# A two-layer hybrid decoder step on one core: the front part of a layer reordered on ScalarE, VectorE and GpSimd

## The chip, the cores and the metric

The kernel runs on one core of one Trainium2 chip. The metric is the device time in microseconds (us) of one execution of the whole program. Before the change the median of three runs is 1627.45 us (1622.06 to 1631.64). PE is TensorE's matmul stream, PEld its weight loads, DVE is VectorE, ACT is ScalarE, POOL is GpSimd, SP is SyncE.

## What is computed

A token stream of 256 prompt tokens and 8 sequences of 8 sample tokens (T = 320 columns together) passes through two layers. Each layer normalises, projects, runs three mixers side by side, merges them under sigmoid gates, and ends in a SwiGLU block:

```python
z = rms_norm(x) @ w_in            # xr | cq | ckv | kpe | u | v | merge gates
# recurrence (RG-LRU)
r, i = sigmoid(xc @ wa + ba), sigmoid(xc @ wx + bx)        # xc: 4-tap convolution of xr
log_a = -8 * r * softplus(-lam); a = exp(log_a)
h[t] = a * h[t-1] + sqrt(-expm1(2 * log_a)) * (i * xc)
# latent attention
q = rms_norm(cq) @ w_uq; q_nope = rms_norm(...); q_pe = rope(rms_norm(...))
latent = rms_norm(ckv); k_pe = rope(rms_norm(kpe)); k_nope, v = expand(latent)
p = softmax((q_nope.k_nope + q_pe.k_pe) * scale)           # prompt: causal; sample: 16 pages of 128 cached rows
# spatial gating
s = tril(w_s) @ layer_norm(gelu(v)); y = gelu(u) * s        # gelu by tanh
x = x + sum(sigmoid(g) * proj(branch)) @ w_out; x = x + swiglu(rms_norm(x))
```

gelu's tanh argument is sqrt(2/pi) * (x + 0.044715 x^3).

## The kernel before

Activations are held feature-major, 128 partitions by T columns a tile. Nearly all products are made from high and low halves (three matmuls for one), so every streamed weight unit (`raw`, 128x1024) is first copied to `w_hi` on ACT (`split` in the ACT program) and subtracted into `w_lo` on DVE (`split` in the DVE program), in three rotating slots. A unit of 24 matmuls of 320 columns takes PE some 3.6 us; the weights come over SP's queue.

The order on each engine is written out by hand. Each engine has a program of its own, waits on semaphores (`wait_ge`) and raises them (`then_inc`), and runs strictly in its own order. PSUM has eight banks; PE takes a bank once whoever reads it has released it (`release`, a drain and an increment).

A layer runs through these stages: `project` (19 weight units, the normalisations, the gates of the recurrence, query and key products), `spatial_and_attention_inputs`, `prompt_attention` (8 heads, the spatial product between them), `pages` (8 sample sequences over 16 pages, a loop, the longest stage), then the merge rounds and the FFN. "Front part" below means the first three. In layer 0 they take 0 to 149 us of the span, in layer 1 815 to 953 us, and a landmark of layer 1 lies 804.3 us behind that of layer 0.

What the change touches, in the order of the front part (lines of the kernel before, as the profile gives them; every ACT instruction is recorded under the helper's line 1303, and ACT's release under 1307, DVE's under 1754):

- ACT, `project`: after `split(12)` come the latent's high half `lat_hi`, `split(13)` to `split(16)`, `recurrence_tanh(0..3)` (two tanh of 320 columns out of banks 4 to 7, each with a release), `query_tile` (copy and square out of PSUM, banks 1, 2, 3, 0), two rotary tiles, the gelu square and tanh of v (`ge`), the recurrence's second tanh and exponential (`mu`, `tr`), a table load, `split(17)`, `split(18)`, the two logarithms of the recurrence, the logarithms and roots of the query norms (`qrs`), the recurrence's square root (`mu`), and the square of the centred v (`varsq`). Then, in the next stage, the four key copies (`kT`, `ksq`).
- DVE: `split`, `scaled` (PSUM times the token's scale, and a release), the rotary key (L1872 to L1876), the input of the recurrence (L1878), v's gelu (L1882), the floor of the recurrence's tanh at 1e-30 (L1884, `lru_clamped`), the difference of logarithms (L1890), the centring (L1893), the scaled queries `qz` (L1902), the recurrence with its scan (L1908 to L1924), the copy of the absorbed queries `qabs` (L1928), the rotary query scaled (L1934) and rotated (L1941 to L1946), the scaled keys (L1948).
- POOL: gelu's argument in two steps (`gelu_argument`, L634 and L636), once for v and once for u; the split of the key weights into `comb_hi` and `comb_lo` (L643, L645), output DMAs, clearing `qz` (L656), copies of identity and mask (L663, L665), half of the rotary queries by head `qpz` (L672), the masking of the new scores (L687, L690).
- PE at the end of `project`: key products (L908), the sum of squares of v (L835, `var_mm`), the absorbed queries (L921, banks 4 and 5, `abs_mm`), the sums of squared keys (L928, `kstat`, banks 0 to 3), the rotation of the queries (L934, banks 4 and 5, `qrot_mm`), the value products (L942), the new scores (L961). In `prompt_attention` L1019 transposes the probabilities that DVE has normalised (L1999 to L2002).

## Time and profile before

| | us | share of the span |
|---|---|---|
| median of three runs | 1627.45 | |
| the profiled execution, its own time | 1621.21 | |
| its span, first to last instruction | 1619.4 | |
| PE busy | 1573.2 | 97% |
| PEld busy | 1522.0 | 94% |
| DVE busy | 1061.5 | 66% |
| ACT busy | 885.0 | 55% |
| POOL busy | 532.2 | 33% |

In forty slices of the span PE is busy nine tenths or more nearly everywhere; the slices below that are the first (7 tenths) and the ones from 121 to 162 us and from 931 to 972 us (8 tenths each). Matmuls are pipelined, so "busy" is not "at its peak": a small hesitation between two of them can hide in it. In a timeline a row is a run of equal instructions, with its start, how long it took, its count, and in brackets the idle time of its engine before it and who ended it.

### The profile page before, as it was taken

The page shows a single profiled execution, that of the slowest core. Times are in us where ns is not written, and L with a number is a line of the kernel's source. Part 1 is how long each engine was busy: PE and PEld are TensorE (multiplying, and loading weights), DVE is VectorE, ACT ScalarE, POOL GpSimd, SP SyncE. Part 2 cuts the span into 40 slices and gives each one's busy share as a digit, 9 for nine tenths or more (in the row PEclk, how much of TensorE's full clock was granted, in tenths as well). Part 3 has the DMA queues.
Part 4 walks back from the last instruction along what each step waited for, and adds up shares of the span by engine and source line. Part 5 has one row for each costly group of instructions (what it writes and reads, how often), then busy time and mean ns, then how long its engine had stood idle before and what let it go on. Part 6 is the DMA issues. An engine that isn't in the chain of part 4 may idle for free. (4 is left out here: it accounts for less than half of the span.)

```text
span 1619.4 us, 33228 instructions
## 1 busy us (share of the span) xinstructions
PE 1573.2 (97%) x10860; PEld 1522.0 (94%) x10860; DVE 1061.5 (66%) x1619; ACT 885.0 (55%) x1612; POOL 532.2 (33%) x667
## 2 busy tenths in 40 slices
PE   7998999999999999999999989999999999999999
PEld 7877999999899999999998779999998999999999
DVE  6586767777555766664375867677775647666633
ACT  5676676667533454443357766766774344544432
POOL 3742367776520000000048413777675000000000
PEclk9999999999999999999999999999999999999999
DMA  7331455554544444444453314555535344444443
GB/s 269 117 106 40 130 183 157 161 158 125 157 141 146 146 154 144 154 147 154 143 192 96 103 57 135 184 156 162 161 115 172 125 156 146 148 149 151 147 150 116
DMA packets 114690, 232.90 MB, mean 144 GB/s; under 512 B 12881, under 2 KB 78706, under 8 KB 114450
## 3 DMA queue, kind: packets, MB, share of 16 engines
q1 hardware_dynamic: 112178, 223.13, 44.4%
q0 software_dynamic: 2400, 8.36, 1.5%
q8 instruction: 60, 0.98, 0.3%
q14 instruction: 52, 0.43, 0.1%
HBM read 228.98 MB, written 2.46 MB: 143 GB/s over the span
## 5 line engine op out<-in xcount | busy, mean ns | idle before, releaser
L1760 DVE TENSOR_TENSOR w_lo<-raw,w_hi 128x1024 fp32r<-128x1024 f32 x258 | 319.4, 1240 | 236.9 <-ACT w_hi L1303 234.5
L1303 ACT ACTIVATE w_hi<-raw 128x1024 fp32r<-128x1024 f32 x258 | 272.0, 1056 | 336.4 <-PE PS L808 322.3
L808 PE MATMUL PS<-h_hi,w_hi 128*128 128x320 f32 x1360 | 427.4, 314 | 9.8 <-DVE h_lo L1787 8.8
L808 PE MATMUL PS<-h_hi,w_lo 128*128 128x320 f32 x1360 | 422.6, 311 | 0.0
L808 PE MATMUL PS<-h_lo,w_hi 128*128 128x320 f32 x1360 | 422.3, 311 | 0.0
L808 PEld LDWEIGHTS PS<-h_hi,w_hi 128*128 128x128 f32 x1360 | 257.5, 189 | 14.2 <-issue 7.9
L808 PEld LDWEIGHTS PS<-h_lo,w_hi 128*128 128x128 f32 x1360 | 257.4, 189 | 0.8
L808 PEld LDWEIGHTS PS<-h_hi,w_lo 128*128 128x128 f32 x1360 | 257.2, 189 | 0.0
L1303 ACT ACTIVATE ksqp<-PS 128x512 f32<-128x512 f32 x256 | 153.2, 599 | 160.1 <-PE PS L1053 158.0
L1053 PE MATMUL PS<-comb_hi,lt_hi 128*128 128x288 f32 x1024 | 239.9, 315 | 0.0
L2106 DVE TENSOR_REDUCE kss<-ksqp 128x8 f32<-128x512 f32 x256 | 174.2, 682 | 99.3 <-ACT ksqp L1303 98.6
L1053 PE MATMUL PS<-comb_hi,lt_lo 128*128 128x288 f32 x1024 | 218.6, 294 | 0.0
L1053 PE MATMUL PS<-comb_lo,lt_hi 128*128 128x288 f32 x1024 | 218.5, 294 | 0.0
L745 POOL TENSOR_TENSOR r_lo<-rrow,r_hi 128x512 fp32r<-128x512 f32 x128 | 167.9, 1316 | 59.9 <-ACT r_hi L1303 35.3
L717 POOL TENSOR_TENSOR lt_hi<-tpage,lt_hi 64x256 fp32r<-64x256 f32 x128 | 116.7, 911 | 147.3 <-ACT lt_hi L1303 140.5
L1053 PEld LDWEIGHTS PS<-comb_lo,lt_hi 128*128 128x128 f32 x1024 | 164.0, 188 | 0.0
L1053 PEld LDWEIGHTS PS<-comb_hi,lt_lo 128*128 128x128 f32 x1024 | 163.8, 188 | 0.0
L1053 PEld LDWEIGHTS PS<-comb_hi,lt_hi 128*128 128x128 f32 x1024 | 158.8, 189 | 0.0
L1763 DVE TENSOR_TENSOR lt_lo<-tpage,lt_hi 128x512 fp32r<-128x512 f32 x128 | 108.1, 845 | 27.0 <-ACT lt_hi L1303 27.0
L808 PE MATMUL PS<-hid_hi,w_lo 128*128 (+1 forms) x352 | 108.8, 309 | 0.0
L808 PE MATMUL PS<-hid_lo,w_hi 128*128 (+1 forms) x352 | 108.8, 309 | 0.0
L808 PE MATMUL PS<-hid_hi,w_hi 128*128 (+1 forms) x352 | 108.8, 309 | 0.0
(317 smaller groups left out, 2678.5 us busy)
## 6 DMA issues: line engine op xcount, KB each, us to landing
raw<-in_stream SPq DMA_DIRECT2D x258, 512.0 KB, 3.5
tpage<-in_tcache SPq DMA_DIRECT2D x256, 192.0 KB, 2.4
rrow<-in_rcache SPq DMA_DIRECT2D x256, 128.0 KB, 2.5
x<-in_xT SPq DMA_DIRECT2D x2, 640.0 KB, 5.7
sbias<-in_sbias POOLq DMA_DIRECT2D x2, 640.0 KB, 7.1
out_yT<-x SPq DMA_DIRECT2D x4, 320.0 KB, 2.2
const<-in_consts SPq DMA_DIRECT2D x1, 1088.0 KB
wgate<-in_wgate POOLq DMA_DIRECT2D x2, 512.0 KB, 5.0
```

What stands on the lines that cost most here:

```text
L717: nc.gpsimd.tensor_tensor(half, tpage[64:128, c % TBUF, :, 256:384], f(half), ALU.subtract).then_inc(pt_rope.sem, 1)
L745: nc.gpsimd.tensor_tensor(r_lo[:, at, :], rrow[:, src, :], f(r_hi[:, at, 0:KVL]), ALU.subtract).then_inc(rows_split.sem, 1)
L808: done = mm(out, w[:, slot, c], a, start=first and n == 0 and m == 0, stop=last and n == len(pairs) - 1 and m == 2)
L1053: last = mm(PS[:, 2 * s + g, c0:c0 + 288], a[:, t, i, 128 * k:128 * k + 128], w[:, k, g, c0:c0 + 288], start=k == 0 and n == 0, stop=k == ...
L1303: return nc.scalar.activation(out, in_, func, **kw)
L1760: V.tensor_tensor(w_lo[:, s, :], raw[:, s, :], f(w_hi[:, s, :]), ALU.subtract).then_inc(lo_done.sem, 1)
L1763: return V.tensor_tensor(out, whole, f(hi_), ALU.subtract)
L2106: V.tensor_reduce(kss[:, par, p, :], ksqp[:, s, :].rearrange("p (h c) -> p h c", h=H), AX.X, ALU.add).then_inc(pk_ss.sem, 1)
```

## The change

Nothing of what is computed changes beyond rounding: the floor of the recurrence (a maximum with 1e-30, then the logarithm of twice the value) becomes a bias of 2e-30 inside that logarithm, and gelu's argument is formed as (x^2 + 1/0.044715) * x with the constant moved into the tanh's scale. The parts:

1. ACT runs `recurrence_tanh(0)` ahead of `lat_hi` and `split(14)`; `split(14)` and `split(15)` follow each other; the two first query tiles come before v's square; two more tiles come ahead of `recurrence_tanh(2)`; `split(16)` and the rotary tiles come ahead of `recurrence_tanh(3)`; `split(17)` and `split(18)` move ahead of the recurrence's second tanh; the query norms (logarithms and both roots) move ahead of the recurrence's logarithms; `y0_hi` moves behind the keys' roots.
2. DVE forms both gelu arguments with one instruction each (v's behind `split(15)`, u's behind `normalised(1)` in the prompt attention); the rotary key moves ahead of `split(16)`; the floor goes; the centring moves ahead of the difference of logarithms; the queries' scaling and rotation move into and ahead of the scan; the keys' scaling moves ahead of `y0_lo`.
3. POOL loses both gelu arguments; its half of `qpz` comes first, then identity and mask (with a signal of their own), then the two output DMAs; the masking of the new scores also waits for the second normalised head. The rows of v get a semaphore of their own.
4. PE rotates the queries first, then sums v's squares, then the squared keys, and makes the absorbed queries last.
5. Scratch `srs` lies in `wk_raw` instead of the score buffer.

```diff
-GELU_C = float(np.sqrt(2.0 / np.pi))
+GELU_C = float(np.sqrt(2.0 / np.pi)) * 0.044715
+GELU_A = 1.0 / 0.044715
...
-    srs = sp_[:, 0, 0:T]
+    tiny_t = small[:, 46:47]
+    srs = wk_raw[:].rearrange("p k j c -> p (k j c)")[:, 0:T]
...
@@ gpsimd
-                nc.gpsimd.tensor_scalar(ge[:], ge[:], 0.044715, 1.0, ALU.mult, ALU.add)
-                pool.drain()
-                nc.gpsimd.tensor_tensor(ge[:], ge[:], src[:], ALU.mult).then_inc(garg.sem, 1)
-
-            gelu_argument(0, va)
...
-            pool.wait_ge(lru_h.sem, lru_h.at(l, 1))
...
-            pool.wait_ge(abs_mm.sem, abs_mm.at(l, 1))
-            pool.sem_inc(waits_passed, 1)
-            nc.gpsimd.tensor_copy(ident_r[:], cst("ident"))
-            pool.drain()
-            nc.gpsimd.tensor_copy(mask_r[:], cst("mask"))
-            pool.drain()
             pool.wait_ge(qpe_ready.sem, qpe_ready.at(l, 1))
...
             pool.drain().then_inc(qpz_ready.sem, 1)
+            pool.wait_ge(abs_mm.sem, abs_mm.at(l, 1))
+            pool.sem_inc(waits_passed, 1)
+            nc.gpsimd.tensor_copy(ident_r[:], cst("ident"))
+            pool.drain()
+            nc.gpsimd.tensor_copy(mask_r[:], cst("mask")).then_inc(qpz_ready.sem, 1)
+            pool.drain()
+            pool.wait_ge(lru_h.sem, lru_h.at(l, 1))
...
-            gelu_argument(1, ua)
...
             pool.wait_ge(sn_copied.sem, sn_copied.at(l, 1))
+            pool.sem_inc(waits_passed, 1)
+            pool.wait_ge(ps_prob.sem, ps_prob.at(l, 2))
@@ tensor
+            pe.wait_ge(qn_ready.sem, qn_ready.at(l, 2))
+            for j in range(2):
+                pe.wait_ge(bank_free[4 + j].sem, banks.take(l, 4 + j))
+                mm(PS[:, 4 + j, 0:T], cst("rot"), qpe[:, j, :], start=True, stop=True).then_inc(qrot_mm.sem, 1)
+
             pe.wait_ge(bank_free[6].sem, banks.take(l, 6))
             pe.wait_ge(varsq.sem, varsq.at(l, 1))
             grouped(PS[:, 6, 0:T], ones[:], [ge[:, j, :] for j in range(4)]).then_inc(var_mm.sem, 1)
+
+            pe.wait_ge(kT_copied.sem, kT_copied.at(l, 4))
+            for j in range(4):
+                pe.wait_ge(bank_free[j].sem, banks.take(l, j))
+                last = mm(PS[:, j, 0:T], cst("blk64"), ksq[:, j, :], start=True, stop=True)
+            last.then_inc(kstat.sem, 1)
...
-            pe.wait_ge(qpz_ready.sem, qpz_ready.at(l, 2))
+            pe.wait_ge(qpz_ready.sem, qpz_ready.at(l, 3))
@@ scalar
+            split(l, 13)
+            act.wait_ge(params.sem, params.at(l, 1))
+            recurrence_tanh(0)
+            act.wait_ge(cscaled.sem, cscaled.at(l, 2))
+            A(lat_hi[:], lat[:], ACT.Copy).then_inc(chi.sem, 1)
+            split(l, 14)
+            split(l, 15)
+            recurrence_tanh(1)
+            query_tile(0, 1)
+            query_tile(1, 2)
+            act.wait_ge(z_scaled.sem, z_scaled.at(l, 13))
+            A(ge[:], va[:], ACT.Square).then_inc(gsq.sem, 1)
+            query_tile(2, 3)
+            query_tile(3, 0)
+            recurrence_tanh(2)
+            split(l, 16)
+            rotary_query_tile(0, 1)
+            rotary_query_tile(1, 2)
+            recurrence_tanh(3)
             act.wait_ge(garg.sem, garg.at(l, 1))
             A(ge[:], ge[:], ACT.Tanh, scale=GELU_C).then_inc(gth.sem, 1)
+            split(l, 17)
+            split(l, 18)
...
-            act.wait_ge(lru_gated.sem, lru_gated.at(l, 1))
-            act.wait_ge(lru_clamped.sem, lru_clamped.at(l, 1))
-            act.wait_ge(gelu.sem, gelu.at(l, 1))
-            A(ge[:], mu[:], ACT.Ln, bias=ones[:, 0:1])
-            A(mu[:], mu[:], ACT.Ln, scale=2.0)
-            act.drain().then_inc(lru_logs.sem, 1)
...
             root(tmp8[:, 4:8, :]).then_inc(qrs.sem, 1)
+            root(tmp8[:, 0:2, :]).then_inc(qrs.sem, 1)
+            act.wait_ge(gelu.sem, gelu.at(l, 1))
+            A(ge[:], mu[:], ACT.Ln, bias=ones[:, 0:1])
+            A(mu[:], mu[:], ACT.Ln, scale=2.0, bias=tiny_t)
+            act.drain().then_inc(lru_logs.sem, 1)
@@ vector
             split(l, 15)
-
-            split(l, 16)
+            dve.wait_ge(gsq.sem, gsq.at(l, 1))
+            V.scalar_tensor_tensor(ge[:], ge[:], GELU_A, va[:], ALU.add, ALU.mult).then_inc(garg.sem, 1)
...
-            dve.wait_ge(lra.sem, lra.at(l, 1))
-            V.tensor_scalar_max(mu[:], mu[:], 1e-30).then_inc(lru_clamped.sem, 1)
...
+            scaled(l, 17, 2, ua[:, 2, :])
+            dve.wait_ge(lru_logs.sem, lru_logs.at(l, 1))
+            V.tensor_tensor(mu[:], mu[:], ge[:], ALU.subtract).then_inc(lru_diff.sem, 1)
             scaled(l, 18, 3, ua[:, 3, :])
+            dve.wait_ge(qrs.sem, qrs.at(l, 2))
+            V.scalar_tensor_tensor(qpe[:], qpe[:], v("qr_g"), tmp8[:, 0:2, :], ALU.mult, ALU.mult).then_inc(qn_ready.sem, 1)
...
             normalised(1)
+            dve.wait_ge(gsq.sem, gsq.at(l, 2))
+            V.scalar_tensor_tensor(ge[:], ge[:], GELU_A, ua[:], ALU.add, ALU.mult).then_inc(garg.sem, 1)
```

## Rows read from the trace of the kernel before

**Rows 1.** The page, part 1: busy time, share of the span, instructions.
```profile
PE 1573.2 (97%) x10860; PEld 1522.0 (94%) x10860; DVE 1061.5 (66%) x1619; ACT 885.0 (55%) x1612; POOL 532.2 (33%) x667
```

**Rows 2.** Waits of PE over the span: total us, times, longest us.
```profile
PE PS L1019 <- DVE sp_ L2002: 8.8, 6, 2.5
...
PE PS L889 <- DVEq L1754: 2.9, 2, 1.7
PE PS L934 <- DVE qpe L1934: 2.8, 2, 1.6
PE PS L808 <- ACTq L1307: 2.4, 2, 1.2
...
PE PS L961 <- POOLq L673: 0.7, 2, 0.3
```

**Rows 3.** Timeline of PE, layer 0: start, us, instruction, count, idle before.
```profile
56.30 1.24 PE L864 MATMUL PS<-xc,wgate 128*128 128x320 f32 x4
...
98.30 1.95 PE L921 MATMUL PS<-qz,wkT 128*128 128x128 f32 x16
100.08 2.32 PE L928 MATMUL PS<-ksq,const 128*128 128x320 f32 x8
104.01 1.34 PE L934 MATMUL PS<-qpe,const 128*128 128x320 f32 x4 [1.61 <-DVE qpe L1934]
105.19 3.60 PE L942 MATMUL PS<-wv_first,lat 128*128 128x512 f32 x8
...
111.09 1.04 PE L961 MATMUL PS<-qpz,kpe 128*64 128x512 f32 x2 [0.35 <-POOLq L673]
...
120.68 0.55 PE L1019 MATMUL PS<-const,sp_ 128*128 128x128 f32 x3 [1.63 <-DVE sp_ L2002]
...
142.33 0.90 PE L1019 MATMUL PS<-const,sp_ 128*128 128x128 f32 x3 [2.52 <-DVE sp_ L2002]
```

**Rows 4.** Timeline of ACT, layer 0, same columns.
```profile
54.84 1.05 ACT L1303 ACTIVATE w_hi<-raw 128x1024 fp32r<-128x1024 f32 x1
58.73 0.74 ACT L1303 ACTIVATE lat_hi<-lat 128x640 fp32r<-128x640 f32 x1 [2.85 <-DVE lat L1859]
...
63.57 1.28 ACT L1303 ACTIVATE ge<-va 128x1280 f32<-128x1280 f32 x1 [0.67 <-DVE va L1793]
...
87.63 2.01 ACT L1303 ACTIVATE tmp<-PS,small 128x1280 f32<-128x1280 f32 x2
89.94 1.27 ACT L1303 ACTIVATE tmp<-tmp 128x1280 f32<-128x1280 f32 x1 [0.30 <-issue]
...
95.10 0.44 ACT L1303 ACTIVATE kT<-PS 128x320 f32<-128x320 f32 x1 [0.92 <-DVE qz L1902]
...
98.25 0.43 ACT L1303 ACTIVATE ksq<-PS 128x320 f32<-128x320 f32 x1
```

**Rows 5.** Timeline of DVE, layer 0, same columns.
```profile
91.95 3.11 DVE L1902 SCALAR_TENSOR_TENSOR qz<-qn,small,tmp 64x1280 f32<-64x1280 f32 x2 [0.21 <-issue]
...
117.00 1.43 DVE L1988 TENSOR_SCALAR pst<-pst 128x2 f32<-128x2 f32 x1
...
119.40 1.05 DVE L2001 TENSOR_SCALAR sp_<-sp_,pst 128x128 f32<-128x128 f32 x1
...
125.09 1.49 DVE L1969 TENSOR_TENSOR va<-PS,sbias 128x1280 f32<-128x1280 f32 x1 [2.98 <-PE PS L983]
```

**Rows 6.** Tile ge, a DVE instruction of gelu: ns min/median/max, first and last start.
```profile
L1882 DVE SCALAR_TENSOR_TENSOR va<-ge,va x2: 1483/1484/1486, 78.6 to 883.5; 128x1280 f32<-128x1280 f32 x2
```

**Rows 7.** Timeline of POOL, layer 0: the argument for u, the masking of the new scores.
```profile
115.50 2.90 POOL L636 TENSOR_TENSOR ge<-ge,ua 128x1280 f32<-128x1280 f32 x1 [1.90 <-ACT va L1303]
...
119.27 1.09 POOL L687 TENSOR_SCALAR_AFFINE_SELECT snew<-snew 64x512 f32<-64x512 f32 x1
```

**Rows 8.** Timeline of POOL, layer 0: the low half of the key weights.
```profile
81.08 2.41 POOL L645 TENSOR_TENSOR comb_lo<-wk_raw,comb_hi 128x1024 fp32r<-128x1024 f32 x1
```

**Rows 9.** Busy time by stretch; after PE, PEld, DVE, ACT, POOL: granted PE clock.
```profile
142.00:146.00 4.00, 3.67 (x13) 2.13 (x14) 1.75 (x7) 1.59 (x5) 0.00 (x0) 0.57 0.00 0
```

More of the change, by code:

```diff
@@ L1423, in query_tile, with rotary_query_tile @@
                 release(bank)
[L1425 to L1442 removed]
+            def rotary_query_tile(m, bank):
                 if m < 1:
@@ L1876, in project @@
             V.tensor_tensor(kpe[:], kpe[:], rt[:, 1, :], ALU.add).then_inc(kpe_ready.sem, 1)
+            split(l, 16)
             dve.wait_ge(lgate.sem, lgate.at(l, 8))
```

85 lines of the change are left out of this document (24 added, 61 removed).

## The prediction

> **What bounds the kernel now.** I read the page first: PE is busy 97% of the span [rows 1], so a change on the other engines can only win what PE idles, and everything behind a win moves up with it (the pages, merge and FFN stages keep PE fed whatever they start from). Second, PE's waits [rows 2]: summed over both layers the front part's are 2.4 us for ACT's release of a query bank, 2.9 for DVE's release of bank 4, 2.8 for the scaled rotary queries and 0.7 for the queries by head. The 8.8 us for normalised probabilities are six waits, three in each layer. Third, the timeline of PE with its idle times [rows 3]: in layer 0 the three last of them are 1.61 us before the rotation, 0.35 before the new scores, 1.63 before the first transposed head, and 2.52 before the seventh. The last repeats in layer 1. An idle time counts from the modelled end of a matmul, though the next could have started about 0.15 us before that end, so a wait that goes brings its row and some 0.15 us. Then I followed ACT and DVE back from these waits [rows 4, 5].
>
> **The change, part by part, for one layer.** I work in layer 0's times; layer 1 is the same 804.3 us later.
>
> *Banks in the middle of `project`.* The early query tiles free banks 1 and 2 before PE has ended the first query unit, and the rotary key ahead of `split(16)` frees bank 4 as soon as PE has filled it. Both waits go (2.4 and 2.9 us over both layers, [rows 2]). PE reaches the key products some 3 us earlier. Whether it keeps this is decided behind them, by ACT.
>
> *ACT up to the key copies.* From the end of `split(13)` (54.84 + 1.05 = 55.9) to the last squared key (98.25 + 0.43 = 98.7) ACT has the same instructions before and after, in another order. So only its waits differ. Before they are 2.85 + 0.67 + 0.92 = 4.4 us [rows 4]. After, the first tanh waits for the gate product: PE starts the pair at 56.3, the first is done about 57.0 [rows 3], a wait of 1.1. The second new wait is for DVE. The queries' root is done at 89.94 + 1.27 = 91.2 before; it gains 2.85 + 0.67 - 1.1 = 2.4 of waits, and the recurrence's two logarithms (2.6 us, which end where the row at 87.63 starts) now stand behind it: 91.2 - 2.4 - 2.6 = 86.2. DVE then scales the queries (3.1 us, [rows 5]), takes one `scaled` (0.6) and the difference of logarithms (1.5, a 1280-wide instruction as in [rows 6]): 91.4. ACT has been free since 86.2 + 0.65 + 2.6 = 89.4: a wait of 2.0. The last squared key is done at 98.7 - 4.4 + 1.1 + 2.0 = 97.4; with drains I take 97.6.
>
> *PE behind the key products.* New order: rotation, v's squares, squared keys, absorbed queries. PE would be at the squared keys at about 96.3 and finds them at 97.65: **a new idle time of about 1.3 us** in place of the 1.61 at the rotation. From there 2.16 + 1.78 us for squared keys and absorbed queries (spacings of starts, [rows 3]; with no wait between, the squared keys take 2.16) bring the value products to 101.6, where they were at 105.19: **3.6 us earlier**. Most of the 3 us won in `project` is in this, not beside it. DVE must have rotated the queries by then: their scale is there at about 93, the recurrence's square root at 92.6, the rotation product at 94.3, so DVE frees banks 4 and 5 near 96.3, ahead of the absorbed queries at 99.8. Cover 3.5 us.
>
> *New scores.* Before they wait 0.35 us for POOL [rows 3]. After, the rotary queries are ready near 98, POOL's half of `qpz` by 101, ACT's by 106.2, the keys by 105.6; PE comes at 107.1. The wait goes, **0.5 us** with the overlap.
>
> *Gelu's arguments.* POOL's two steps give way to one DVE instruction of 1.5 us each [rows 6]. v's falls where DVE only waited for `split(16)`; u's where DVE idles 2.98 us for the spatial product [rows 5]: both cost nothing on PE's path. If that cover were gone the second would cost 1.5 us. What goes is more. L1988 works on two columns and took 1.43 us at 117.00; it ended at 118.43, POOL's argument for u at 118.40. L2001 took 1.05 us and ended at 120.45, POOL's masking at 120.36 [rows 5, 7]. DVE stood still behind POOL for some 1.3 + 0.8 = 2.1 us, right ahead of the first normalised head, for which PE waited 1.63. The change takes the first away and puts the masking behind the second head. **1.63 + 0.15 = 1.8 us**, of which I count 1.5, since DVE then ends only 0.1 to 0.3 us ahead of PE.
>
> A rule speaks against part of this. The Trainium skill (SBUF — State Buffer, Who interferes with whom) says that a DVE instruction with two SBUF inputs and a GpSimd instruction that reads SBUF exclude each other for the whole instruction. By it the new arguments, `split(17)` and `split(18)` meet POOL's key weights. The rows of 117.00 and 119.40 agree that DVE waits for POOL's end. Without the page: if `comb_hi` and `comb_lo` (2.41 us, [rows 8]) hold DVE up in full, `split(18)` is done at 82.2, and PE wants it at 85.9; the scan is held up by 1.3 us by `qpz`, and ACT wants its result 0.8 us later than that. So the sum stays, but it names where it would break.
>
> *The rest.* The floor goes off DVE, where it was covered. The masking now waits for the second head; behind it on POOL stand the first two sequences' queries and the first rotary split, wanted only at the pages (149 us), 20 us later. The outputs `hlast` and `convn` and the row DMA move by a few us; SP's page loads wait for the first two, but also for `latnew`, which is later. The wait of 2.52 us at the seventh head stays, and with it the low clock behind it: 0.57 granted over 142 to 146 us, where 1.2 GHz was granted instead of 2.4 for most of it [rows 9].
>
> *Sum.* 3.6 + 0.5 + 1.5 = 5.6 us a layer, **11.2 us** in all. Against the profiled execution: 1621.2 - 11.2 = 1610.0. That execution lies 6.2 us below the median of 1627.45 and under all three runs shown, so the forecast of the median is 1627.45 - 11.2 = **1616.2 us**.
>
> **Bounds.** Nothing in the trace shows ACT's new order. If its chain is 1.3 us shorter, the new idle time vanishes: 12.9 + some overlap, 14 us saved at most. If ACT or DVE is 1.5 us later (a locked DVE in front of `qz`, drains), each layer loses 1.5. The attention's 1.5 lies between 0 and 1.8.
>
> **Rivals.**
> (a) *ACT is the new bound, and late.* For it: from the first tanh to the key copies ACT has only two waits left, and PE already stands 1.3 us for it. Against: same instructions. With 1.5 us more a layer and half of the attention's gain (0.75): 2 x (1.5 + 0.75) = 4.5 less, 6.7 saved, 1620.8.
> (b) *The front's lead is handed back at the attention.* Spatial rows (`va`) are ready only when ACT has done `q128`, `latnew` and the four scalings; they end near 111.6 and PE wants them at 112.1, so a delay over 0.5 us costs in full. With 2 us late and no gain at the heads: 11.2 - 2 x (1.5 + 1.5) = 5.2 saved, 1622.2.
> (c) *Slower: the clock.* The wait of 2.52 us at the seventh head is followed by the granted clock of 0.57 [rows 3, 9], the one of 1.63 is not (full clock). If the new wait at the squared keys grows past about 2 us (ACT late by 0.7), the clock may fall there too: some 3.4 us at half clock, 1.7 lost. That alone leaves a gain. It ends slower only from ACT 4 us late: 5.6 - 4 - 1.7 = -0.1 a layer; at 5 us late 1.1 us a layer, 2.2 in all, 1629.7. Nothing in the trace points to 4 us.
> (d) *The change does not take the locks away*: the 2.1 us at the heads come from DVE itself. Then 11.2 - 3.0 = 8.2 saved, 1619.2. Against: the two ends agree within 0.1 us.
>
> **How the numbers follow.** Forecast (9 to 14 saved) 0.6; (a) 0.15; (b) 0.08; (d) 0.1; (c) and anything slower 0.07. A measurement of this kernel can tell 0.5%, 8.1 us, from no change. The forecast is beyond it, (d) lies on it, (a) and (b) within. Faster 0.64, same 0.31, slower 0.05. The range takes in 14 saved (1613.5) and (b) (1622.2), widened by the scatter of the runs shown, about 4 us to either side: 1609 to 1626.
>
> **What the profile after would show.** Right: no wait of PE at L808 for ACT's release, none for bank 4; one idle time of 1 to 1.5 us at the squared keys; no wait at the rotation and the new scores; the two-column L1988 near 0.17 us throughout and no wait at the first transposed head; the wait of 2.5 us at the seventh head still there; pages beginning near 143 us instead of 148.5, and twice that lead at the end. Wrong: an idle time over 2.5 us at the squared keys (ACT's chain), waits of PE for `w_lo` of units 17 and 18 (the lock at the key weights), or a wait at the spatial transposes.

## The result, and the profile after

| | before | after |
|---|---|---|
| median, us | 1625.51 (4 runs, 1622.06 to 1631.64) | 1607.23 (4 runs, 1606.92 to 1612.2) |
| ratio, 95% interval | 1 | 0.9899 (0.9873 to 0.9926) |
| the profiled execution, own time / span | 1621.21 / 1619.4 | 1607.19 / 1605.4 |
| mean granted clock over the runs | 0.9938 | 0.9968 |
| span times granted clock, mean of the runs | 1613.9 | 1601.4 |

The change makes the kernel 18.3 us faster. The last row is an estimate of what a run would take at full clock throughout; I call it the full-clock time. By it 12.5 us of the 18.3 come from less waiting (0.001 of mean granted clock is 1.6 us here). The before column of the two clock rows is taken over 26 runs made later, with a median of 1624.63: 0.9 us of the 18.3 is the difference of the two medians of before, and 4.9 are left for a clock that is granted in full more of the time.

This estimate gives the clock too much. Within one kernel the time falls by 1.22 us for each 0.001 of granted clock, not by 1.6 (a line fitted to all 131 runs of this study, each kernel about its own mean; 95% interval 1.14 to 1.31). By this slope, which is an estimate too, the 17.4 us between the means of the 26 runs and of the four are 13.8 of waiting and 3.6 of clock. Where two kernels' clocks differ by 0.001, the difference of their full-clock times is off by some 0.4 us; below, the figure by the slope is given beside it where that matters.

The busy time of each engine has hardly moved, except POOL's:

```profile
PE 1568.4 (98%) x10860; PEld 1520.4 (95%) x10860; DVE 1061.1 (66%) x1622; ACT 884.7 (55%) x1612; POOL 521.9 (33%) x659
```

The waits of PE over the span (total us, times, longest) have other names than those of [rows 2]. In the code after, L859 is the gate product, L919 the squared keys, L984 the first product of a head's scores, L1014 the transposes.

```profile
PE PS L1014 <- DVE sp_ L1992: 5.5, 4, 2.5
PE PS L859 <- issue: 1.8, 2, 1.3
PE PS L984 <- DVEq L1750: 1.4, 2, 0.7
...
PE PS L919 <- ACTq L1488: 0.4, 1, 0.4
```

The waits at L808 and L889, for ACT's and DVE's release of banks, are gone, as are those for the scaled rotary queries and for the queries by head. The 8.8 us for normalised probabilities are 5.5, and four times instead of six. Three new lines stand there: 1.8 at a gate product, 1.4 at a head's scores, 0.4 at the squared keys. PE's timeline of layer 0 puts them in their place (start, us, instruction, count, idle before):

```profile
67.96 1.31 PE L859 MATMUL PS<-xc,wgate 128*128 128x320 f32 x4 [0.54 <-issue]
...
96.39 2.42 PE L919 MATMUL PS<-ksq,const 128*128 128x320 f32 x8 [0.36 <-ACTq L1488]
98.64 1.95 PE L927 MATMUL PS<-qz,wkT 128*128 128x128 f32 x16
100.43 3.60 PE L937 MATMUL PS<-wv_first,lat 128*128 128x512 f32 x8
...
109.88 0.44 PE L984 MATMUL PS<-mask_r,ident_r 128*128 128x384 f32 x1 [0.69 <-DVEq L1750]
...
114.27 0.49 PE L1014 MATMUL PS<-const,sp_ 128*128 128x128 f32 x3
...
135.84 0.55 PE L1014 MATMUL PS<-const,sp_ 128*128 128x128 f32 x3 [2.52 <-DVE sp_ L1992]
```

The first transposed head (114.27) waits for nothing, and 0.2 us in layer 1; the seventh (135.84) waits its old 2.52 us. A layer's first gate product starts 1.2 us earlier here than in [rows 3] (55.10 against 56.30), though nothing ahead of it was changed; over all kernels of this study it starts between 55.1 and 58.1 us in layer 0. So I count from this product, in each layer:

| us after the layer's first gate product, layer 0 / layer 1 | before | after | earlier by |
|---|---|---|---|
| squared keys | 43.78 / 44.20 | 41.29 / 41.38 | 2.5 / 2.8 |
| value products | 48.89 / 48.87 | 45.33 / 45.32 | 3.56 / 3.55 |
| new scores | 54.79 / 54.77 | 50.46 / 50.44 | 4.33 / 4.33 |
| first transposed head | 64.38 / 64.32 | 59.17 / 59.38 | 5.21 / 4.94 |
| pages | 92.24 / 91.94 | 85.56 / 86.82 | 6.68 / 5.12 |

Up to the first transposed head the two layers win 10.15 us. The rest lies behind it, and the clock shows in it. Before, the clock is low behind the wait of 2.52 us in both layers: 0.57 over 142 to 146 us [rows 9], 0.79 over 946 to 954 us. After, the same wait is followed by full clock in layer 0 and by a low one in layer 1 (columns: window, length, then busy us of PE, PEld, DVE, ACT, POOL, granted clock, DMA share, GB/s):

```profile
135.00:143.00 8.00, 5.60 (x36) 4.38 (x37) 3.75 (x12) 4.00 (x9) 1.75 (x5) 1.00 0.00 1
...
932.00:944.00 12.00, 10.41 (x47) 8.87 (x46) 3.39 (x8) 4.10 (x10) 1.75 (x5) 0.57 0.11 34
```

ACT's timeline of layer 0 has the two waits that were forecast, before the table load ahead of the first tanh (L1298 at 55.88) and before the recurrence's square root (90.41):

```profile
55.88 1.28 ACT L1298 ACT_TABLE_LOAD   x1 [1.20 <-PE PS L859]
...
83.81 1.90 ACT L1298 ACTIVATE tmp<-tmp 128x1280 f32<-128x1280 f32 x2 [0.31 <-issue]
85.61 1.35 ACT L1298 ACTIVATE ge<-mu,ones 128x1280 f32<-128x1280 f32 x1
86.87 1.35 ACT L1298 ACTIVATE mu<-mu,small 128x1280 f32<-128x1280 f32 x1
90.41 1.27 ACT L1298 ACTIVATE mu<-mu 128x1280 f32<-128x1280 f32 x1 [2.20 <-DVE mu L1896]
```

DVE's timeline of layer 0: the new argument for v, the splits of units 17 and 18, the scan, the two-column instruction and the argument for u.

```profile
65.45 1.49 DVE L1865 SCALAR_TENSOR_TENSOR ge<-ge,va 128x1280 f32<-128x1280 f32 x1 [0.75 <-ACT ge L1298]
...
75.46 2.06 DVE L1756 TENSOR_TENSOR w_lo<-raw,w_hi 128x1024 fp32r<-128x1024 f32 x1
...
78.06 2.80 DVE L1756 TENSOR_TENSOR w_lo<-raw,w_hi 128x1024 fp32r<-128x1024 f32 x1
...
96.60 3.91 DVE L1921 TENSOR_TENSOR_SCAN ti<-tr,ti 128x320 f32<-128x320 f32 x4
...
112.38 0.17 DVE L1978 TENSOR_SCALAR pst<-pst 128x2 f32<-128x2 f32 x1
...
115.95 1.49 DVE L1998 SCALAR_TENSOR_TENSOR ge<-ge,ua 128x1280 f32<-128x1280 f32 x1
```

The two-column instruction takes 0.17 us where it took 1.43 [rows 5]. POOL's timeline of layer 0 shows where it waits now instead: its conv step at 65.50 takes 1.63 us, the same step 0.32 a column tile before. DVE's argument for v runs from 65.45 to 66.94, and the step ends at 67.13; in layer 1 the steps beside `split(15)` and the argument take 1.43 us for 0.39, and 2.62 for 1.27.

```profile
59.86 0.32 POOL L618 TENSOR_TENSOR mu<-mu 128x64 f32<-128x64 f32 x1
...
65.50 1.63 POOL L618 TENSOR_TENSOR mu<-mu 128x64 f32<-128x64 f32 x1
...
97.20 1.92 POOL L656 COPY qpz<-qpe 32x640 f32<-32x640 f32 x2 [13.52 <-DVE qpe L1919]
```

### The profile page after: what moved, and what is told of

Its sections match the earlier page's. It is cut to its first block, busy times and chain, and to the rows that moved or that the text cites. A ratio compares the mean times of both kernels' runs of the same rounds, so it can differ in the third digit from the quotient of the medians.

```text
span 1605.4 us, 33213 instructions
## 1 busy us (share of the span) xinstructions
PE 1568.4 (98%) x10860; PEld 1520.4 (95%) x10860; DVE 1061.1 (66%) x1622; ACT 884.7 (55%) x1612; POOL 521.9 (33%) x659
## 3 DMA queue, kind: packets, MB, share of 16 engines
HBM read 228.98 MB, written 2.46 MB: 144 GB/s over the span
## 4 chain that ended last, share of the span: by engine, by line
PE 90%; DVE 3%; ACT 3%; issue 2%; DVEq 1%; POOLq 1%; ACTq 1%; DMA 0%; POOL 0%; SPq 0%
PE PS L803 53%; PE PS L1048 26%; PE PS L1081 2%; PE PS L1082 2%; PE PS L1043 1%; POOLq L725 1%; ACT w_hi L1298 1%; PE PS L859 1%; PE PS L830 1%; DVEq L1750 1%; DVEq L2040 1%; DVE w_lo L1756 1%; PE PS L988 0%; PE PS L987 0%; PE PS L1063 0%
## 5 line engine op out<-in xcount | busy, mean ns | idle before, releaser
L1756 DVE TENSOR_TENSOR w_lo<-raw,w_hi 128x1024 fp32r<-128x1024 f32 x258 | 323.5, 1255 | 219.8 <-ACT w_hi L1298 216.5
L1298 ACT ACTIVATE w_hi<-raw 128x1024 fp32r<-128x1024 f32 x258 | 271.9, 1056 | 335.4 <-PE PS L803 319.9
L1298 ACT ACTIVATE ksqp<-PS 128x512 f32<-128x512 f32 x256 | 153.3, 599 | 161.2 <-PE PS L1048 159.1
```

Of the source, the lines that this page charges most:

```text
L1298: return nc.scalar.activation(out, in_, func, **kw)
L1756: V.tensor_tensor(w_lo[:, s, :], raw[:, s, :], f(w_hi[:, s, :]), ALU.subtract).then_inc(lo_done.sem, 1)
```

## The experiments

Each kernel ran beside the kernel before on the same chip. "Full clock" is the estimate of above, in means over the runs; the last two columns are one profiled execution each, layer 0 / layer 1, us after the first gate product.

| kernel | median us (runs) | ratio (95%) | granted clock | full clock | new scores | first transposed head |
|---|---|---|---|---|---|---|
| before | 1624.6 (26), 1626.5 (11), 1626.0 (17) | 1 | 0.9938, 0.9936, 0.9935 | 1613.9, 1614.6, 1613.8 | 54.8 / 54.8 | 64.4 / 64.3 |
| after | 1607.23 (4) | 0.9899 (0.9873 to 0.9926) | 0.9968 | 1601.4 | 50.5 / 50.4 | 59.2 / 59.4 |
| after_again | 1608.77 (4) | 0.9893 (0.987 to 0.9917) | 0.9968 | 1601.7 | 50.4 / 50.4 | 59.1 / 59.4 |
| gelu_only | 1615.26 (10) | 0.9942 (0.9924 to 0.9959) | 0.9975 | 1610.3 | 54.8 / 54.9 | 62.6 / 62.7 |
| gelu_back | 1618.34 (10) | 0.9952 (0.9927 to 0.9977) | 0.9954 | 1608.7 | 51.3 / 52.2 | 61.6 / 62.4 |
| rotation_last | 1619.18 (10) | 0.9961 (0.9943 to 0.9979) | 0.9938 | 1607.8 | 54.3 / 54.6 | 63.6 / 63.8 |
| rot_last_masks | 1610.15 (4) | 0.9901 (0.9873 to 0.9929) | 0.9972 | 1604.0 | 52.2 / 52.2 | 60.0 / 60.0 |
| middle_back | 1611.76 (4) | 0.9911 (0.9883 to 0.9939) | 0.9988 | 1608.0 | 52.7 / 52.9 | 61.5 / 61.8 |
| logs_first | 1613.23 (4) | 0.9912 (0.9886 to 0.9938) | 0.9952 | 1602.7 | 50.7 / 50.7 | 59.8 / 60.0 |
| y2_late | 1607.98 (5) | 0.99 (0.9868 to 0.9933) | 0.9968 | 1601.3 | 50.4 / 50.5 | 59.2 / 59.4 |
| latent_first | 1605.04 (4) | 0.9866 (0.9838 to 0.9894) | 0.9985 | 1602.1 | 50.5 / 50.5 | 59.0 / 58.7 |
| all_three | 1604.94 (6) | 0.9869 (0.9848 to 0.989) | 0.9982 | 1600.2 | 50.4 / 50.4 | 58.9 / 58.6 |
| head_wait | 1619.61 (12) | 0.996 (0.9944 to 0.9976) | 0.9922 | 1605.0 | 50.4 / 50.4 | 61.6 / 61.3 |

**gelu_only: the arguments alone, in the kernel before.** The kernel before with both arguments on DVE and the masking behind the second head; the rest of the change is left out.

```diff
@@ gpsimd
-            gelu_argument(0, va)
...
-            gelu_argument(1, ua)
...
+            pool.wait_ge(ps_prob.sem, ps_prob.at(l, 2))
+            pool.sem_inc(waits_passed, 1)
@@ vector
             split(l, 15)
+            dve.wait_ge(gsq.sem, gsq.at(l, 1))
+            V.scalar_tensor_tensor(ge[:], ge[:], GELU_A, va[:], ALU.add, ALU.mult).then_inc(garg.sem, 1)
...
             normalised(1)
+            dve.wait_ge(gsq.sem, gsq.at(l, 2))
+            V.scalar_tensor_tensor(ge[:], ge[:], GELU_A, ua[:], ALU.add, ALU.mult).then_inc(garg.sem, 1)
```

> The kernel before, with only gelu's two arguments on VectorE and the masking of the new scores behind the second normalised head; no other order changed. Theory (VectorE stands still behind GpSimd): the wait of PE at the first transposed head (1.63 and 1.58 us) goes to nothing, the two-column L1988 falls from 1.43 to 0.17 us; in layer 1 PE's wait for bank 4 falls from 1.73 to about 1.14 us, since split(16) is no longer held up; the other waits of the front part stay. In all about 4 us saved, ratio near 0.9975. Rival (those waits are VectorE's own work): the wait at the first head stays at 1.6 us or grows with the added instruction, ratio 0.999 to 1.002.

DVE's and PE's timelines, layer 0: the two-column instruction is short, and ahead of the heads only the old waits of [rows 3] are left.

```profile
117.02 0.17 DVE L1982 TENSOR_SCALAR pst<-pst 128x2 f32<-128x2 f32 x1
```
```profile
104.03 1.34 PE L927 MATMUL PS<-qpe,const 128*128 128x320 f32 x4 [1.60 <-DVE qpe L1928]
```

The first transposed head comes 1.80 and 1.63 us earlier (64.38 to 62.58, 64.32 to 62.69), and nothing ahead of it moves. So DVE's standstill behind POOL was the whole of that wait, and rival (d) falls. The first scaling of the normalised head, too, takes 0.29 us where L2001 took 1.05 [rows 5]; no run moves the argument for u and the masking one by one. In layer 1 the wait for bank 4 falls from 1.73 to 1.1 us, as expected, and the one at the rotation grows from 1.17 to 1.61: what PE wins ahead of it is handed back there. The time fell by 9.4 us, though, where 4 were expected. These two heads are 3.4 of it, and the full-clock time fell by 3.6 (5.1 by the slope): the granted clock rose from 0.9938 to 0.9975, worth the rest.

**gelu_back: the change without the arguments.** In the kernel after, both arguments go back to POOL as before, and the masking loses its second wait.

```diff
@@ gpsimd
+            gelu_argument(0, va)
...
+            gelu_argument(1, ua)
...
-            pool.wait_ge(ps_prob.sem, ps_prob.at(l, 2))
-            pool.sem_inc(waits_passed, 1)
@@ vector
-            V.scalar_tensor_tensor(ge[:], ge[:], GELU_A, va[:], ALU.add, ALU.mult).then_inc(garg.sem, 1)
...
-            V.scalar_tensor_tensor(ge[:], ge[:], GELU_A, ua[:], ALU.add, ALU.mult).then_inc(garg.sem, 1)
```

> The changed kernel with both gelu arguments back on GpSimd in two steps, and the masking not waiting for the second head. Theory: in the new order ScalarE wants v's argument 3 us before GpSimd has it, and ScalarE's chain sets PE's start of the squared keys, so PE loses 2 to 3.5 us a layer there; at the first head the wait is back with 0.5 to 1.6 us. In all 5 to 10 us slower than the changed kernel (some 1613 to 1617 us, ratio 0.993 to 0.997). Rival (the order alone makes the gain, the place of the arguments is neutral): within 2 us of the changed kernel.

PE's timeline, layer 0 (L918 is the rotation, L927 the squared keys, L1022 the transposes):

```profile
93.53 1.34 PE L918 MATMUL PS<-qpe,const 128*128 128x320 f32 x4 [0.80 <-DVE qpe L1905]
98.05 2.42 PE L927 MATMUL PS<-ksq,const 128*128 128x320 f32 x8 [1.00 <-ACTq L1496]
...
117.58 0.55 PE L1022 MATMUL PS<-const,sp_ 128*128 128x128 f32 x3 [1.49 <-DVE sp_ L1998]
```

The wait at the first head is back in layer 0 (1.49). In layer 1 it is not; there PE waits 1.04 us for ACT's release at a head's scores. The squared keys come 0.8 and 1.6 us later (42.09 and 43.01 us instead of 41.3), where 2 to 3.5 were expected, and a wait of 0.80 and 0.98 at the rotation was not expected. v's argument on POOL is part of the chain of ACT and DVE to the key copies: without it on DVE the new scores are 0.8 and 1.7 us later. The time rises by 11 us over the kernel after, 7.3 at full clock (8.0 by the slope); 5 to 10 were expected.

**rotation_last: the rotated queries back to their place.** The rotation stands last on PE and on DVE, as before, and the absorbed queries ahead of the squared keys; the other moves stay.

```diff
@@ tensor
-            pe.wait_ge(qn_ready.sem, qn_ready.at(l, 2))
-            for j in range(2):
-                pe.wait_ge(bank_free[4 + j].sem, banks.take(l, 4 + j))
-                mm(PS[:, 4 + j, 0:T], cst("rot"), qpe[:, j, :], start=True, stop=True).then_inc(qrot_mm.sem, 1)
-
             pe.wait_ge(bank_free[6].sem, banks.take(l, 6))
...
+                last = mm(PS[:, j, 0:T], cst("blk64"), ksq[:, j, :], start=True, stop=True)
+            last.then_inc(kstat.sem, 1)
+
+            pe.wait_ge(qn_ready.sem, qn_ready.at(l, 2))
...
@@ vector
             V.memset(first_a, 0.0)
-            dve.wait_ge(qrot_mm.sem, qrot_mm.at(l, 2))
...
                 release(b)
+            dve.wait_ge(qrot_mm.sem, qrot_mm.at(l, 2))
...
```

> The changed kernel with the rotated queries last again: PE makes v's squares, absorbed queries, squared keys, rotation; VectorE rotates behind the absorbed copy, as before. Theory (ScalarE's chain sets the lead, not PE's order): the rotation finds its operand ready, since VectorE now scales the rotary queries ahead of the recurrence; no wait of 1.6 us comes back; new scores and what follows move by less than 1 us a layer, 0 to 2 us in all. Rival (the new PE order is what removed the 2.8 us of waits at the rotation): 3 us or more slower than the changed kernel.

PE's timeline at the new scores, layer 0, and POOL's ahead of it (L656 is its half of the queries by head, L660 the identity, L662 the mask):

```profile
110.01 1.04 PE L956 MATMUL PS<-qpz,kpe 128*64 128x512 f32 x2 [3.60 <-POOL mask_r L662]
```
```profile
104.35 3.38 POOL L656 COPY qpz<-qpe 32x640 f32<-32x640 f32 x2 [20.11 <-DVE qpe L1933]
108.00 1.23 POOL L660 CAST ident_r<-const 128x128 fp32r<-128x128 f32 x1 [0.26 <-issue]
109.36 0.51 POOL L662 CAST mask_r<-const 128x384 fp32r<-128x384 f32 x1
```

The value products are where they are in the kernel after, or 0.2 us earlier in layer 0 (45.13 and 45.40 us). Behind them PE waits 3.60 us for POOL, in both layers, and the new scores come 3.8 and 4.1 us later. The time rises by 12 us over the kernel after, 6.4 at full clock (7.7 by the slope), where 0 to 2 were expected. This miss is the largest of the study: I had taken the order of the rotation as nearly free. POOL's copy takes 3.38 us instead of 1.92 (DVE is then in its 1280-wide instructions on keys and `y_lo`), and identity and mask stand behind it in POOL's queue.

**rot_last_masks: the same with identity and mask ahead.** It tells POOL's queue from the lock.

```diff
@@ gpsimd
+            pool.wait_ge(abs_mm.sem, abs_mm.at(l, 1))
+            pool.sem_inc(waits_passed, 1)
+            nc.gpsimd.tensor_copy(ident_r[:], cst("ident"))
+            pool.drain()
+            nc.gpsimd.tensor_copy(mask_r[:], cst("mask")).then_inc(qpz_ready.sem, 1)
+            pool.drain()
             pool.wait_ge(qpe_ready.sem, qpe_ready.at(l, 1))
...
             pool.drain().then_inc(qpz_ready.sem, 1)
-            pool.wait_ge(abs_mm.sem, abs_mm.at(l, 1))
...
```

> The kernel with the rotation last, which waited 3.6 us for GpSimd before the new scores, with one thing changed: GpSimd copies identity and mask ahead of the queries by head, as in the kernel before the change. Theory (GpSimd's queue): the two copies, 1.7 us behind the queries by head, leave the path, and the wait falls from 3.6 to about 2 us; what is left is the copy itself, held up by VectorE (3.38 us there, 1.92 in the changed kernel), until about 1.7 us later than in the changed kernel. Rival (the late rotation itself, not GpSimd): the wait stays at 3.6 us.

The wait at the new scores falls from 3.60 to 1.52 us. The new scores come 2.1 and 2.4 us earlier than in rotation_last: that part is POOL's queue, identity and mask behind the copy. They are still 1.7 us later than in the kernel after: that part is that the queries are rotated late and copied against DVE (3.65 us for 1.92). The time is within the intervals of the kernel after (0.9901 against 0.9899), 2.6 us more at full clock.

**middle_back: the middle of `project` as before.** ACT's order of tanh, query tiles, v's square and splits 14 to 16 goes back; DVE and PE keep theirs.

```diff
             split(l, 13)
-            act.wait_ge(params.sem, params.at(l, 1))
-            recurrence_tanh(0)
...
             split(l, 14)
+            act.wait_ge(params.sem, params.at(l, 1))
+            recurrence_tanh(0)
+            act.wait_ge(z_scaled.sem, z_scaled.at(l, 13))
+            A(ge[:], va[:], ACT.Square).then_inc(gsq.sem, 1)
             split(l, 15)
...
-            act.wait_ge(z_scaled.sem, z_scaled.at(l, 13))
-            A(ge[:], va[:], ACT.Square).then_inc(gsq.sem, 1)
+            recurrence_tanh(2)
             query_tile(2, 3)
             query_tile(3, 0)
-            recurrence_tanh(2)
+            recurrence_tanh(3)
             split(l, 16)
...
-            recurrence_tanh(3)
```

> The changed kernel with only ScalarE's order from split(13) to the last gate tanh put back (latent's high half and split(14) first, v's square early, third gate tanh ahead of the third query tile, split(16) last). Theory (PE's lead behind the key products is ScalarE's chain, and the change only took waits out of it): ScalarE waits 2.9 and 0.7 us again instead of 1.2, so the squared keys, and all behind them, come 2 to 2.5 us later in each layer; PE's waits for query banks (1.2 us) return, but inside that, not beside it. 4 to 5 us over the changed kernel at full clock. Rival (the bank waits count beside the chain): 3.5 us or more a layer. Rival (the middle order is hidden): under 1 us a layer.

PE's timeline, layer 0:

```profile
67.39 0.39 PE L803 MATMUL PS<-cq_hi,w_hi 128*128 128x320 f32 x1 [1.18 <-ACTq L1302]
75.50 0.81 PE L884 MATMUL PS<-tmp,const 128*128 128x320 f32 x2 [0.99 <-ACTq L1427]
...
99.36 2.42 PE L919 MATMUL PS<-ksq,const 128*128 128x320 f32 x8 [0.88 <-ACTq L1488]
```

The wait for a query bank (1.18 and 1.34 us) is back; at L884 PE waits 0.99 us for ACT's release of a bank, where it waited for DVE's before the change. The squared keys come at 43.6 us and the new scores 2.28 and 2.46 us later. The reorder of ACT is worth 2.4 us a layer, by ACT's chain to the squared keys: PE still waits 0.88 us for it. At full clock 6.6 us are lost (5.9 by the slope), more than the 4 to 5 expected and the 4.7 that the new scores show; the clock (0.9988 in four runs, the highest of all kernels) gives back some 2.

**logs_first: the recurrence's logarithms ahead of the query norms.** It undoes the one move that sends ACT into the wait of 2.20 us.

```diff
@@ scalar
             log_and_exp_tables()
+            act.drain()
+            act.wait_ge(gelu.sem, gelu.at(l, 1))
+            A(ge[:], mu[:], ACT.Ln, bias=ones[:, 0:1])
+            A(mu[:], mu[:], ACT.Ln, scale=2.0, bias=tiny_t)
+            act.drain().then_inc(lru_logs.sem, 1)
             act.wait_ge(qstat.sem, qstat.at(l, 1))
...
             root(tmp8[:, 0:2, :]).then_inc(qrs.sem, 1)
-            act.wait_ge(gelu.sem, gelu.at(l, 1))
...
@@ vector
+            dve.wait_ge(lru_logs.sem, lru_logs.at(l, 1))
+            V.tensor_tensor(mu[:], mu[:], ge[:], ALU.subtract).then_inc(lru_diff.sem, 1)
             dve.wait_ge(mean_mm.sem, mean_mm.at(l, 1))
...
             scaled(l, 17, 2, ua[:, 2, :])
-            dve.wait_ge(lru_logs.sem, lru_logs.at(l, 1))
...
```

> The changed kernel with the recurrence's two logarithms ahead of the query norms on ScalarE, and their difference ahead of the centring on VectorE, as before the change. Theory (only ScalarE's waits count): the norms come 2.6 us later, but ScalarE no longer waits 2.2 us for the difference; PE gets a wait of about 0.4 us at the rotation and loses its wait at the squared keys; the new scores move by under 0.5 us. Rival (the early norms are what moved the squared keys forward, as the forecast's sum took them): squared keys 2 us or more later in each layer.

ACT waits no more for the difference, and the new scores move by 0.2 us only (50.66 in both layers): the 2.6 us that the queries win by going first are paid back in the wait of 2.20. PE's timeline of layer 0 shows where the rest is paid:

```profile
92.45 0.41 PE L903 MATMUL PS<-lat_hi,comb_hi 128*128 128x320 f32 x1 [0.77 <-DVEq L1751]
...
111.36 0.44 PE L984 MATMUL PS<-mask_r,ident_r 128*128 128x384 f32 x1 [1.12 <-DVEq L1751]
```

A key product waits 0.77 us (1.50 in layer 1) for a bank that DVE releases with `scaled`, behind the queries' scaling, and the second head's scores 1.12 instead of 0.69. The first transposed head is 0.65 us later in each layer. The median is 4.5 us over after_again, 1.0 of it at full clock (1.6 by the slope) and the rest a mean clock of 0.9952 in four runs, which the expectation did not cover.

**y2_late, latent_first, all_three: are the new waits on the path?** y2_late: DVE makes `y2_lo` behind the seventh head instead of ahead of it. latent_first: ACT and DVE make the latents of the new rows, which release bank 1, ahead of `q128` and its low half. all_three: both, and DVE's argument for v also waits for POOL's convolution.

```diff
@@ y2_late, vector
+            normalised(6)
             dve.wait_ge(y2h.sem, y2h.at(l, 1))
             lo(y2_lo[:], va[:], y2_hi[:]).then_inc(y2_ready.sem, 1)
-            normalised(6)
@@ latent_first, scalar
-            act.wait_ge(sel_mm.sem, sel_mm.at(l, 1))
-            for jt in range(2):
...
             act.wait_ge(latT_mm.sem, latT_mm.at(l, 1))
...
             act.drain().then_inc(latnew_ready.sem, 1)
+            act.wait_ge(sel_mm.sem, sel_mm.at(l, 1))
+            for jt in range(2):
...
@@ latent_first, vector
+            dve.wait_ge(latnew_ready.sem, latnew_ready.at(l, 1))
+            low = latnew[TS:2 * TS, 0:KVL]
+            lo(low, PS[TS:2 * TS, 1, 0:KVL], low).then_inc(latnew_ready.sem, 1)
+            release(1)
             dve.wait_ge(q128_hi.sem, q128_hi.at(l, 1))
...
             release(6)
-            dve.wait_ge(latnew_ready.sem, latnew_ready.at(l, 1))
...
@@ all_three, vector, with both of these
             split(l, 15)
+            dve.wait_ge(conv_sample.sem, conv_sample.at(l, 4))
             dve.wait_ge(gsq.sem, gsq.at(l, 1))
```

> The changed kernel with VectorE's low half of the spatial rows behind the seventh normalised head instead of ahead of it. PE's wait of 2.52 us before the seventh transposed head shrinks to about 1.1 us; part of it comes back at the eighth. From the waits alone 1 to 3 us saved in all against the changed kernel. If the low clock is released by that idle time, the stretches at half the clock near the end of the prompt attention are gone too, which is worth 1.7 us for each 3.4 us at half the clock: 1601 to 1605 us. If it is not, they stay.

> The changed kernel with the new latent's copy and low half ahead of the spread rotary queries, on ScalarE and on VectorE, so that bank 1 is released 1.5 us or more earlier. Theory: PE's wait of 0.69 us before the second head's scores (for VectorE's release of bank 1) goes, and the new scores to the first transposed head take 8.0 to 8.3 us instead of 8.7 to 8.9, 1.2 us saved in both layers. Rival (the rows of v are next): the same 0.5 us comes back as a wait at the spatial transposes.

> The changed kernel with three additions: latent first as in latent_first; v's gelu argument on VectorE waits until GpSimd has ended the sample convolution; the low half of the spatial rows behind the seventh head. Theory: 1.2 us from the latent, 0 from the convolution (its wait of 0.5 and 1.3 us goes, but ScalarE's chain still sets the squared keys, where a wait of 1 us shows up instead), 1.1 us from the seventh head; 2 to 2.5 us under the changed kernel at full clock, and fewer stretches at half clock: 1602 to 1606 us. Rival (the convolution's wait counts in full): 1.8 us more.

PE's timeline of all_three, layer 0:

```profile
96.78 2.42 PE L919 MATMUL PS<-ksq,const 128*128 128x320 f32 x8 [1.00 <-ACTq L1488]
...
111.57 1.50 PE L967 MATMUL PS<-const,va 128*128 128x128 f32 x12 [0.52 <-ACT va L1298]
...
134.63 0.55 PE L1014 MATMUL PS<-const,sp_ 128*128 128x128 f32 x3 [1.11 <-DVE sp_ L1993]
136.73 0.55 PE L1014 MATMUL PS<-const,sp_ 128*128 128x128 f32 x3 [0.76 <-DVE sp_ L1993]
```

The wait at the gate product is gone, the one at the squared keys is 1.00 us in both layers, and the new scores stand where they did (50.43). So the waits of 0.54 and 1.28 at the gates cost nothing: ACT's chain sets the squared keys at 41.26, and whatever PE loses ahead of it comes out of this wait. The wait for bank 1 (0.69) is gone too, and 0.52 comes back at the spatial transposes behind it, for the scaled rows of v; the first head is 0.2 and 0.8 us earlier. The wait of 2.52 us becomes 1.11 and 0.76 at the head behind it. The pages begin 84.75 and 84.45 us after the gates, against 85.53 and 87.07 in after_again. With latent_first this is the fastest median of the study (1604.94 and 1605.04), about 3 us below the kernel after, but the intervals of the ratios overlap: that it is faster is likely and not shown. At full clock latent_first gains nothing (1602.1 against 1601.4), though its first head comes 0.2 and 0.7 us earlier (1.2 in all were expected); all_three gains 1.2 us (1.7 by the slope), where 2 to 2.5 were expected.

y2_late alone leaves the time where it was: 1607.98, and 1601 to 1605 were expected. Its waits at the seventh and eighth head are 1.12 and 0.76 us, so of the 2.52 only 0.6 are won. The expectation had a second part, that the stretches at half clock near the end of the prompt attention go if that wait releases them. They are gone in its profiled execution, in both layers; in layer 0 the seventh head starts at 137.40:

```profile
134.00:142.00 8.00, 5.61 (x32) 3.58 (x30) 5.62 (x17) 5.42 (x15) 0.00 (x0) 1.00 0.16 49
```

The same holds for all_three. Over all profiled executions of this study the granted clock is below full for some microseconds behind the seventh head in 16 of the 22 layers that wait 2.5 us there, and in none of the four in which the wait is shortened. So the low clock at this place goes with this wait. The mean over the runs does not show it: it is 0.9968 in the five runs of y2_late (0.993 to 0.999), as in the kernel after. Five runs with this scatter cannot exclude a gain of 0.002, some 2.5 us.

**head_wait and after_again: the clock.** head_wait is the kernel after with three more copies of the new scores on DVE, ahead of the first normalised head, so that PE waits there about as long as before. after_again is the kernel after, unchanged, beside it.

```diff
             dve.wait_ge(sn_mm.sem, sn_mm.at(l, 1))
+            for _ in range(3):
+                V.tensor_copy(snew[0:TS].rearrange("p b (h t) -> p h b t", h=H),
+                              PS[0:TS, 2, :].rearrange("p (h b t) -> p h b t", h=H, b=NB))
+                dve.drain()
             V.tensor_copy(snew[0:TS].rearrange("p b (h t) -> p h b t", h=H),
```

> The changed kernel, with VectorE copying the new scores out of PSUM four times instead of once ahead of the first normalised head: three times 0.67 us more on VectorE, so that PE waits about 1.8 us for the first transposed head again, as it did before the change (1.63). Theory (that wait lowers the clock): 3.6 us for the two waits, and the mean granted clock falls from about 0.997 to the 0.994 of the kernel before, some 5 us more: 1614 to 1617 us. Rival (the clock does not hang on this wait): 3.6 us and no change of clock, 1610 to 1612 us.

> The changed kernel once more, beside the two others of this call, for its granted clock. Theory (the change also takes stretches at half clock away): mean granted clock over its runs 0.996 to 0.999, against 0.993 to 0.995 for the kernel before on the same chip; time 1605 to 1610 us. Rival (the clock is chance): both kernels' mean clocks within 0.001 of each other.

PE's timeline of head_wait, and the stretch behind that wait, first in head_wait and then in after_again:

```profile
117.43 0.55 PE L1014 MATMUL PS<-const,sp_ 128*128 128x128 f32 x3 [2.32 <-DVE sp_ L1996]
```
```profile
117.00:131.00 14.00, 13.57 (x55) 10.80 (x55) 6.01 (x17) 6.09 (x13) 5.85 (x11) 0.63 0.01 3
```
```profile
117.00:131.00 14.00, 13.72 (x79) 10.44 (x78) 10.82 (x26) 9.76 (x24) 5.93 (x11) 1.00 0.06 21
```

PE was busy for as much of the 14 us (13.6 and 13.7) but did 55 matmuls instead of 79: the granted clock was 0.63 there, most of the stretch at 1.2 GHz instead of 2.4, right behind the wait. In layer 1 the same wait (1.95 us) is followed by full clock. Over twelve runs the mean granted clock is 0.9922 against 0.9968 in the four of after_again, whose 1608.77 us and 0.9968 fall where they were expected. The time rises by 10.8 us, above the 1614 to 1617 expected: 3.3 at full clock and 7.5 by the clock, or some 5 and 5.5 by the slope. The second split fits the trace better, in which the first heads come 2.5 and 1.9 us later. Either way the two waits, 4.3 us together, cost 10.8. Where in the slower runs the clock fell is not shown: the profiled execution, at 0.996, is one of the fastest.

## Why the prediction was right, and where it was not

The forecast said 11.2 us saved and 1616.2; measured are 18.3 and 1607.23, faster as forecast, by more, and 1.8 us below the low end of the range. Of the 9.0 us between, 1.9 are the kernel before itself, whose median came to 1625.51 instead of 1627.45; taken by the ratio, 0.9899 of the 1627.45 that the forecast started from is 1611.0, inside the range. The other 7.1 are 0.9 by which the runs of before differ between the two sets, 1.3 at full clock (12.5 against 11.2) and 4.9 of clock; by the slope 2.6 of waiting and 3.6 of clock. The three terms of the sum end at the first transposed head, and up to there the traces show 10.15 us for 11.2. That the full-clock total comes near the forecast is so in part luck: the heads brought less, and what was won behind them was not in the sum.

- *The banks in the middle* (both waits gone): right. middle_back gives back the one for the query bank. The early rotary key, which was to end the one for bank 4, was undone in no run. That what they win is decided by ACT's chain was right too.
- *ACT up to the key copies*: right, and the best of the forecast. Waits of 1.1 and 2.0 us were worked out, 1.20 and 2.20 measured; the last squared key at 97.4 to 97.6 us, 41.35 after the first gate product with PE's start at it, and it came at 41.29 and 41.38. logs_first shows that the order behind it trades 2.6 us for the 2.2 of the wait.
- *The idle time at the squared keys*: forecast 1.3 us, measured 0.36 and none. PE came later by a new wait at the gate product (0.54 and 1.28 us) that was not foreseen: DVE's new argument for v and `split(15)` hold up POOL's convolution (1.63 us for a step of 0.32), and PE's next gate product needs it. The sum is untouched, since the two waits share one slack; all_three gives 1.00 and the same new scores. That is the rule which the prediction cited from the Trainium skill (SBUF — State Buffer, Who interferes with whom) against this part of the change; it held, at another place than the one I named. The forecast's wording of it (two SBUF inputs) does not cover the two-column L1988 and L2001, which have one tensor input each; that DVE waits there is shown by the ends that agree and by gelu_only. The splits of units 17 and 18 were held up as forecast (2.06 and 2.80 us for 1.22), and PE did not wait for them.
- *Value products 3.6 us earlier*: 3.56 and 3.55. *New scores 0.5 more*: 0.78. Together 4.33 for 4.1.
- *What I counted at nothing*: the order of the rotation. It saves no wait in the sum beyond the 0.5 of the new scores, but rotation_last shows 3.8 to 4.1 us a layer behind it. I had asked what the move gains over the kernel before, not what the other moves would lose without it: with the value products 3.6 us earlier, POOL's half of the queries is next in line. Of the 3.8 to 4.1, 2.1 to 2.4 hang on another part of the change, that POOL copies identity and mask behind the queries; with these ahead (rot_last_masks) the late rotation costs 1.7 us a layer.
- *The first transposed head*: forecast 1.5, measured 0.88 and 0.61. The lock went as said (1.43 us to 0.17, and 1.80 and 1.63 us in gelu_only alone). The missing part is a new wait of 0.69 for bank 1 at the second head's scores: rival (b), that the lead is partly handed back at the attention, in a form that I had not named. I had watched the rows of v; latent_first shows that they are next (0.53 and 0.23 us). With the wait for bank 1 gone the first head gains 0.2 and 0.7 us of the 0.9 and 1.2 that are missing from 1.8; beside the 0.53 and 0.23 some 0.2 a layer stay unaccounted for.
- *The seventh head*: 2.52 us stay, as forecast.
- *The clock*: the step that failed. I took it as a price for a new wait of over 2 us and let the old ones stand at no gain, because the granted clock behind the 1.63 us wait was full in the one execution that I read [rows 3, 9]. It brought 3.6 to 4.9 us. Over many runs the clock rises when the first head's wait goes (gelu_only, 0.9938 to 0.9975, with two arguments and the masking moved) and falls when one like it is put in (head_wait, 0.9968 to 0.9922). Single executions bear it out: low clock behind 1.49 us in layer 0 of gelu_back, behind 2.32 in layer 0 of head_wait, behind 3.60 at the new scores in both layers of rotation_last (0.9938 in ten runs); full clock behind 1.58 and 1.63 in before. That the 2.52 us wait at the seventh head is followed by a low clock was read rightly, and that it stays as well. How much of the clock's gain belongs to which wait stays open, and so does the mean of middle_back.
- *A bound*: with ACT's chain 1.3 us shorter the saving is 11.2 + 2 x 1.3 = 13.8, not 12.9; the 14 of the range covers it.

## What to carry to other kernels

When several engines are late by about as much, a part of a reorder is worth more beside the others than alone: undone one at a time, three parts of this change cost 6.6, 7.3 and 6.4 us at full clock, 20 in all, though the change brings 12.5 (5.9, 8.0 and 7.7 of 13.8 by the slope). The arguments alone, in the kernel before, bring 3.6 (5.1). Some of the 6.4 is a cost that another part of the change sets up (POOL's order). So price an order by asking who is next once the others have moved, and not only by the waits that the trace of before shows. And where a tensor engine is busy nearly throughout, compare the mean granted clock over many runs before and after: one profiled execution does not show what a wait of 2 us costs in clock.

## What the runs showed of the hardware

- DVE and POOL hold each other up, in both directions and in small instructions as well: 1.63 us for a POOL step of 0.32, 3.38 us for a POOL copy of 1.92, 3.91 us for the four scans of DVE that took 2.97 before, 1.43 us for two columns on DVE that take 0.17. The Trainium skill (SBUF — State Buffer, Who interferes with whom) has this as an exclusive lock on a shared port pair. The durations agree with it: the step of 1.63 us and the two-column instruction end within 0.2 us of what held them up.
- Waits of 2.32 and 1.95 us of PE at the first head cost 10.8 us, of which 5.5 to 7.5 by a lower granted clock. The same wait is followed by a low clock in some executions and layers and not in others: behind 2.52 us at the seventh head in 16 layers of 22.
- The first gate product scatters by 3 us between executions of kernels that are equal up to there, so landmarks are to be counted from one behind it.
